# One decoder step on one core: two w_in chunks on tokens without their norm, pre-added squares, and 28 convolution taps placed in the inversion

## The reference, cut to what matters

```python
def rms_norm(x, g):
    xf = x.astype(jnp.float32)
    y = xf * lax.rsqrt(jnp.mean(xf * xf, axis=-1, keepdims=True) + NORM_EPS)
    return (y * g.astype(jnp.float32)).astype(x.dtype)

def conv_group(p, buf, dw_w, dw_b, ln_g, ln_b):
    u = p[..., :CONV_WIDTH] * jax.nn.sigmoid(p[..., CONV_WIDTH:])
    ext = jnp.concatenate([buf.astype(u.dtype), u], axis=1)
    c = lax.conv_general_dilated(ext, dw_w[:, None, :], ...) + dw_b
    ...

def layer(x, mk, mv, prev, s0, buf, lw):
    h = rms_norm(x, lw['g_mix'])
    p = h @ lw['w_in']
    rw, new_prev, new_s = rwkv7_group(p[..., :RW_PROJ], prev, s0, ...)
    cv, new_buf = conv_group(p[..., RW_PROJ:], buf, ...)
    x = x + jnp.concatenate([rw, cv], axis=-1) @ lw['w_out']
    x = x + cross_attn(rms_norm(x, lw['g_xattn']), mk, mv, lw['w_q'], lw['w_o'])
    x = x + moe(rms_norm(x, lw['g_moe']), ...)
    return x, new_prev, new_s, new_buf
```

## Time and profile before

| what | us |
|---|---|
| median of 3 runs | 1334.15 |
| lowest and highest | 1333.44 and 1334.32 |
| the profiled execution | 1333.15 |
| its span, first to last instruction | 1331.4 |
| PE busy / DVE busy / ACT busy | 1276.5 / 405.4 / 190.4 |

### The profile page before, as it was taken

One profiled execution on the slowest core, in us unless ns is written; L12 is line 12 of the kernel. 1 busy time (PEld: TensorE's weight loads), 2 busy tenths in 40 slices (PEclk: granted clock), 3 DMA queues, 4 the chain that ended last, 5 costly groups with the idle time before them and its releaser, 6 DMA issues.

```text
span 1331.4 us, 18885 instructions
## 1 busy us (share of the span) xinstructions
PE 1276.5 (96%) x8184; PEld 635.4 (48%) x8184; DVE 405.4 (30%) x820; ACT 190.4 (14%) x351; POOL 16.1 (1%) x39
## 2 busy tenths in 40 slices
PE   7999999999999999999999999999999999999995
PEld 5777865677784434434344333433333343443332
DVE  3998624532122121221312213112121311212122
ACT  3015222321221000100001000010100000010002
POOL 0002000000000000000000000000000000000000
PEclk9999999999999999999999999999999999999998
DMA  7335131285997999999999999999999999999995
GB/s 251 135 112 133 54 129 64 100 350 198 415 367 313 429 414 427 428 428 427 429 429 427 428 429 428 429 428 428 430 428 429 428 428 429 429 428 428 428 426 206
DMA packets 40280, 464.25 MB, mean 349 GB/s; under 512 B 8528, under 2 KB 10128, under 8 KB 12064
## 3 DMA queue, kind: packets, MB, share of 16 engines
q1 hardware_dynamic: 39392, 459.53, 83.2%
q0 software_dynamic: 832, 3.90, 0.9%
HBM read 458.34 MB, written 5.07 MB: 348 GB/s over the span
## 4 chain that ended last, share of the span: by engine, by line
PE 64%; DMA 26%; DVE 7%; ACT 1%; issue 0%; SPq 0%; DVEq 0%
PE ps L1109 32%; PE ps L567 20%; DMA arena<-in_w_gate 13%; DMA ring<-in_w_gate 10%; PE ps L1177 4%; DVE arena L1499 4%; DMA ring<-in_w_down 2%; PE ps L1133 2%; PE ps L1120 2%; DVE ring L1496 1%; PE ps L1126 1%; PE ps L1211 1%; PE ps L1167 1%; DVE arena L1496 1%; PE ps L1138 1%; DVE ring L1499 1%
## 5 line engine op out<-in xcount | busy, mean ns | idle before, releaser
L1109 PE MATMUL ps<-ring,xT 128*64 128x512 f32 x1536 | 342.7, 596 | 8.3 <-DMA ring<-in_w_up 5.5
L567 PE MATMUL ps<-arena,ring 128*128 128x288 f32 (+2 forms) x1152 | 231.4, 371 | 0.0
L1109 PEld LDWEIGHTS ps<-ring,xT 128*64 128x64 f32 x1536 | 105.9, 137 | 235.1 <-issue 208.4
L567 PEld LDWEIGHTS ps<-arena,ring 128*128 128x128 f32 (+1 forms) x1152 | 179.4, 176 | 45.8 <-issue 4.5
L1109 PE MATMUL ps<-ring,arena 128*64 128x512 f32 x768 | 171.7, 596 | 10.0 <-DMA ring<-in_w_down 10.0
L1253 ACT ACTIVATE arena<-ps 128x512 f32<-128x512 f32 (+5 forms) x136 | 76.3, 569 | 599.3 <-PE ps L1126 330.8
L1109 PE MATMUL ps<-arena,xT 128*64 128x512 f32 x512 | 115.5, 595 | 3.1 <-DMA arena<-in_w_gate 3.1
L1109 PEld LDWEIGHTS ps<-ring,arena 128*64 128x64 f32 x768 | 53.2, 137 | 111.2 <-issue 97.4
L1921 DVE TENSOR_SCALAR xT<-ps 128x512 f32<-128x512 f32 x32 | 22.1, 692 | 185.3 <-PE ps L1109 185.3
L1109 PEld LDWEIGHTS ps<-arena,xT 128*64 128x64 f32 x512 | 35.6, 137 | 74.3 <-issue 66.8
L1876 DVE TENSOR_TENSOR xT<-ps,vec 128x1024 f32<-128x1024 f32 x15 | 18.4, 1225 | 171.6 <-PE ps L1138 171.6
(11 more groups left out here) (218 smaller groups left out, 791.9 us busy)
## 6 DMA issues: line engine op xcount, KB each, us to landing
ring<-in_w_up SPq DMA_DIRECT2D x64, 2048.0 KB, 31.9
ring<-in_w_down SPq DMA_DIRECT2D x47, 2048.0 KB, 31.5
ring<-in_w_gate SPq DMA_DIRECT2D x32, 2048.0 KB, 34.2
arena<-in_w_gate SPq DMA_DIRECT2D x32, 2048.0 KB, 34.3
arena<-in_w_down SPq DMA_DIRECT2D x16, 2048.0 KB, 34.8
ring<-in_w_in SPq DMA_DIRECT2D x4, 2048.0 KB, 12.1
ring<-in_cache_k SPq DMA_DIRECT2D x4, 2048.0 KB, 17.8
ring<-in_cache_v SPq DMA_DIRECT2D x4, 2048.0 KB, 8.7
```

The costliest lines, as they stand in the source:

```text
L567: return nc.tensor.matmul(out, lhsT, rhs, start=start, stop=stop)
L1109: last = nc.tensor.matmul(out[AT[h ^ swap], :], lhs(k), part(weights(i), 0, 4, D)[:, k % 4, h * 512:(h + 1) * 512], start=(fresh and k == ...
```

## The change

- `W_IN_ORDER` begins 14, 15, 18, 19 in place of 14, 18, 15, 19.
- PE starts with twelve products of ones by ones, 128x128, into a bank that nobody reads.
- The first two chunks (14 and 15) are multiplied on `xg`, and `unit(1)` multiplies its gate by the norm's factor as `unit(0)` does.
- DVE adds the squares of the eight slices down to two (`x_sum`, three additions of 128x576), and `squares(1)` is two products in place of eight. It stands after the second product of chunk 15 (`between`). For the memory tokens two additions (128x1024, 128x512) bring eight slices down to two, and `squares(2)` is two products and stands after the third chunk in place of after the first.
- SP loads the weights of the first and second chunk as transfers of their own: chunk 14 goes ahead of the second half of the tokens, then chunk 15, then the other two.
- Taps 17 to 30 of channel blocks 2 and 3 leave their place before `shift(0, 4)` and go into the inversion, after levels 0 to 3: 8, 8, 6 and 6 instructions (`LATE_TAPS`).
- The rest renumbers semaphores. ACT's square for the key norm waits for the 100 convolution steps that then come before it.

The core of the diff:

```diff
+LATE_TAPS = (17, 21, 25, 28, 31)
-W_IN_ORDER = (14, 18, 15, 19, ...)
+W_IN_ORDER = (14, 15, 18, 19, ...)
...
+            for _ in range(12):
+                mm(ps[:, 5, 0:P], ones, ones)
+
-            def squares(n, src, w, bank):
-                pe.wait_ge(S["sq_done"], n)
+            def squares(n, need, src, w, bank):
+                pe.wait_ge(*need)
                 take(bank)
-                for k in range(KT):
+                for k in range(2):
...
-            squares(1, mix, TOK, 6)
...
+                linear("w_in", n, hT, TOK, range(8), "p_ps", 4 * n, p_reader, 4 if n < 5 else 2, steps=("h_done", KT + 2), raw=None if n else xg,
+                       between=lambda: squares(1, (S["h_done"], KT + 1), x_sum, TOK, 6),
+                       after=lambda m: squares(2, (S["mem_h"], 1), mem_sq, MEM, 7) if m == 2 else None)
...
             dve.wait_ge(S["x_in"], 16)
-            dve.wait_ge(S["x_in2"], 32)
-            for k in range(KT):
+            dve.wait_ge(S["piece2"], 16)
+            for k in range(4):
                 tell("h_done", v.tensor_scalar(xg[:, k, :], xT[:, k, 0:TOK], V("g_mix", k), None, MUL), False)
+            dve.wait_ge(S["sq_done"], 1)
+            tell("dve_c", tt(x_sum, mix[:, 0:2, :], mix[:, 2:4, :], ADD), False)
+            dve.wait_ge(S["x_in2"], 16)
+            for k in range(4, KT):
+                tell("h_done", v.tensor_scalar(xg[:, k, :], xT[:, k, 0:TOK], V("g_mix", k), None, MUL), False)
+            dve.wait_ge(S["sq_done"], 2)
+            link(tt(mix[:, 4:6, :], mix[:, 4:6, :], mix[:, 6:8, :], ADD))
+            tell("h_done", tt(x_sum, x_sum, mix[:, 4:6, :], ADD), False)
...
+            dve.wait_ge(S["sq_done"], 3)
+            link(tt(mem_sq[:, 0:4, :], mem_sq[:, 0:4, :], mem_sq[:, 4:8, :], ADD))
+            tell("mem_h", tt(mem_sq[:, 0:2, :], mem_sq[:, 0:2, :], mem_sq[:, 2:4, :], ADD), False)
...
-                if j == 0:
-                    link(tt(tmp2[:, 0, 0:TOK], tmp2[:, 0, 0:TOK], rs[:, :], MUL))
+                if j < 2:
+                    link(tt(tmp2[:, j, 0:TOK], tmp2[:, j, 0:TOK], rs[:, :], MUL))
...
-            conv((2, 3), 0, 17)
+            conv((2, 3), 0, LATE_TAPS[0])
...
-            conv((2, 3), 17, TAPS)
...
                 if 2 <= l + 2 < len(LEVELS):
                     mask_level(l + 2)
+                if l + 1 < len(LATE_TAPS):
+                    conv((2, 3), LATE_TAPS[l], LATE_TAPS[l + 1])
```

More of the change, by code:

```diff
@@ L208, in build @@
         rs_mem = arena[:, 16536:16792]
+        mem_sq = part(arena, 4352, KT, MEM)
+        x_sum = part(arena, 18104, 2, TOK)
         taps_of = [part(arena, at, NB, NT, TAPS) for at in (15544, 16824)]
@@ L567, in mm, with linear @@
                 return nc.tensor.matmul(out, lhsT, rhs, start=start, stop=stop)
-            def linear(name, n, src, width, banks, done, first, reader, tiles=4, steps=None, after=None, raw=None, ready=None):
+            def linear(name, n, src, width, banks, done, first, reader, tiles=4, steps=None, after=None, raw=None, ready=None, between=None):
                 i, f = front_fill(name, n)
                 for m in range(tiles):
-                    if m == 0 and raw is not None:
-                        pe.wait_ge(S["piece0"], 16)
-                    elif m == 0 or m == 1 and raw is not None:
+                    raws = 2 if raw is not None else 0
+                    if m < raws:
+                        pe.wait_ge(S[("piece0", "piece1")[m]], 16)
+                    elif m == raws:
                         pe.wait_ge(slot_in[i], 16 * (f + 1))
@@ L584, in linear @@
                             w = part(ring, i * SLOT, KT, 128 * tiles)[:, k, m * P:(m + 1) * P]
-                        if steps and n == 0 and (m == 0 or m == 1 and raw is not None):
-                            pe.wait_ge(S[steps[0]], steps[1] + m * KT + k)
+                        if m == 0 and raws:
+                            pe.wait_ge(S["h_done"], 1 + k)
+                        if steps and n == 0 and m == raws:
+                            pe.wait_ge(S[steps[0]], steps[1] + k)
                         if ready and first + m == 0 and k in ready:
                             pe.wait_ge(*ready[k])
-                        x = raw if m == 0 and raw is not None else src
+                        x = raw if m < raws else src
                         last = mm(ps[:, b, 0:width], w, x[:, k, 0:width], k == 0, k == KT - 1)
+                        if between and first + m == 1 and k == 1:
+                            between()
                     last.then_inc(S[done], 1)
@@ L596, in _ @@
             pe.wait_ge(S["pool_i"], 1)
-            def squares(n, src, w, bank):
-                pe.wait_ge(S["sq_done"], n)
+            for _ in range(12):
+                mm(ps[:, 5, 0:P], ones, ones)
+            def squares(n, need, src, w, bank):
+                pe.wait_ge(*need)
                 take(bank)
-                for k in range(KT):
-                    last = mm(ps[:, bank, 0:w], ones, src[:, k, :], k == 0, k == KT - 1)
+                for k in range(2):
+                    last = mm(ps[:, bank, 0:w], ones, src[:, k, :], k == 0, k == 1)
                 last.then_inc(S["sum_ps"], 1)
                 readers[bank] = [("root", n)]
-            squares(1, mix, TOK, 6)
             def p_reader(i):
@@ L883, in group_square @@
             def group_square(late):
-                pe.wait_ge(S["sq_done"], 6 if late else 5)
+                pe.wait_ge(S["sq_done"], 7 if late else 6)
                 group_sums(1, late, tsq, 7 if late else 4)
@@ L985, in _ @@
             for n in range(2):
-                linear("w_q", n, hT, TOK, range(8), "q_ps", 4 * n, lambda m: ("q_out", m + 1), steps=("h_done", 2 * KT + 1),
+                linear("w_q", n, hT, TOK, range(8), "q_ps", 4 * n, lambda m: ("q_out", m + 1), steps=("h_done", 2 * KT + 2),
                        after=lambda m: None if m else x_squares())
@@ L1104, in multiply @@
                     if pieces and 4 <= k < 7:
-                        pe.wait_ge(S[f"piece{k - 4}"], r * 16 + (32 if k == 4 else 16))
+                        pe.wait_ge(S[f"piece{k - 4}"], r * 16 + 32)
                     elif k == 0 or k == 4 or pieces and k == 7:
@@ L1257, in _ @@
             act.wait_ge(S["x_in"], 16)
-            a.activation(mix[:, 0:4, :], xT[:, 0:4, 0:TOK], ACT.Square)
-            act.wait_ge(S["x_in2"], 32)
+            tell("sq_done", a.activation(mix[:, 0:4, :], xT[:, 0:4, 0:TOK], ACT.Square), False)
+            act.wait_ge(S["x_in2"], 16)
             tell("sq_done", a.activation(mix[:, 4:, :], xT[:, 4:, 0:TOK], ACT.Square), False)
@@ L1269, in _ @@
             act.wait_ge(S["mem_in"], 16)
-            tell("sq_done", a.activation(part(arena, 4352, KT, MEM), memT, ACT.Square), False)
+            tell("sq_done", a.activation(mem_sq, memT, ACT.Square), False)
             inv_root((S["sum_ps"], 2), rs_mem, ps[:, 7, 0:MEM], 1.0 / D, 0)
@@ L1554, in conv @@
                         tell("conv", last, False)
[L1555 removed]
+                        taps_made[0] += 1
+                        taps_done[c] = taps_made[0]
             def conv_sample(c):
```

28 lines of the change are left out of this document (14 added, 14 removed).

## The result

| | median us | runs | ratio to before, 95% interval |
|---|---|---|---|
| before | 1333.80 | 1333.38 to 1334.32, 4 runs | |
| after | 1353.12 | 1352.58 to 1354.15, 4 runs | 1.0147 [1.0131, 1.0163] |

What follows compares the result with a forecast made beforehand. Full DMA weight stream bounds the end, so only its start, set by PE's and DVE's front, can move: 1333.15 - 8.6 = 1324.5, plus 1.0 for the median, 1325.5 us; range 1324 to 1327.5, with rivals 1323 to 1330 (0.85).

Steps and rivals of the forecast that it cites:

- From that release on, nothing but bytes counts: After PE's first slot release at 406.62 us, the expert weight stream alone sets the time; only its start can move.
- the sum's 1333.15 - 8.6: Whole kernel: profiled execution's time less the earlier lora products' gain, 1324.5 us; median forecast 1325.5.
- my slower rival: PE's new pauses at the start lose the clock; with any other delay, ending above 1334, chance 0.08.
- Early products and the clock: Kernel start: 24 rows of products of ones take 5.3 us and raise the clock, so chunk 14 runs at full pace.
- Rival 1: Start: products of ones don't raise the clock, or late; squares end 2.6 us later, gain 6.0, 1328.1; chance 0.11.
- Rival 4: Start: PE's pauses near 6.4, 8.4, 15.3 and 19.3 us lose the clock; with other delays above 1334, chance 0.08.
- Transfers: First loads: piece 14 at 6.4, second token half at 7.96, piece 15 at 9.3; additional transfer priced at nothing, at most 0.5.
- Start: PE's first chunks: squares end 12.35, norm 14.85, wait 1.2, 19 chunks from 21.4; lora products at 95.2, 8.6 us earlier.
- DVE in time: Up to `prep`: with 28 taps moved, DVE keeps up; `shift(0, 4)` waits until about 80.2; the 0.92 us wait stays.
- both bounds: Up to `prep`: PE's chunks with the small chain behind, and DVE's convolution, almost coincide; unmoved taps would limit the gain to 5.8.
- Taps in the inversion: Tap blocks of 3.2 and 2.4 us fit DVE's idle time, leaving 1.6 to 2.7; priced at nothing, 11.2 if uncovered.
- From `prep` to the release: Stretch before the first slot release: moves along with the earlier front, putting the first release near 398.

Runs made afterwards that it cites:

- before_pad6: The kernel before with six tiny memsets at the start of VectorE's program and nothing of the change: 1362.39 us, ratio 1.0214.
- before_pad7: The kernel before with seven tiny memsets at the start of VectorE's program and nothing of the change: 1334.50 us, ratio 1.0003.
- no_ones: after_pad1 without the 12 products of ones ahead of the first chunk: 1329.55 us.
- after_pad1: The changed kernel with one more tiny memset (128x1, private tile) at the start of VectorE's program: 1328.21 us, ratio 0.9952.
- runs 5 and 6: 5: the kernel before with only the 28 taps spread over the inversion, 1333.64 us; 6: after_pad1 with the 28 taps in their old place, 1328.77 us.
- after_pad1b: Repeat of after_pad1, the changed kernel with one more tiny memset, on another occasion beside other kernels: 1326.16 us.

## Why the prediction was wrong, point by point

- **The end.** "From that release on, nothing but bytes counts" is the step that failed, and with it the sum's 1333.15 - 8.6, which leaves what lies behind the last result as it was. It holds up to the last result (918.9 us after the release in after, 918.6 before). Behind it VectorE's skipped loop costs 27.2 us more, for fetches of code: its head lies across the border of two blocks. I took "what lies around" the work as fixed and moved it along, and counted added instructions by their own duration only. None of the rivals has it; my slower rival named another mechanism.
- **Early products and the clock.** The forecast has chunk 14 at full pace from its first product, since PE has by then worked some 5 us; that is my estimate from the one profile of before, whose squares run at half pace for 4.9 us. Right in after (24 rows in 4.51 us, forecast 5.3; the rows of chunk 14 are 0.24 us apart) and in four of the five other profiles with early products. But the 5 us are one reading of a moment that moves: the record of the clock begins 2.8 to 6.1 us after PE's first product (before_pad6, before_pad7), and the same 24 rows take 4.35 to 5.42 us. Rival 1's price, 2.6, is of the right size: 2.5 in no_ones. In after_pad1 `prep` is 1.95 later than in after, but 0.85 of that is the later piece. Rival 4, the clock lost in pauses, shows in that profile alone, and costs 1.4 and 1.6 us there.
- **Transfers.** First piece in use at 6.37 (forecast 6.4), second token half at 8.47 (7.96): half a us late. In all seven profiles with the new queue it is late, in use at 8.15 to 9.04, so the price of nothing for the additional transfer, or the pace of bytes that I took, is too low by 0.2 to 1.1 us. No run takes that transfer away, so how much of this is its doing stays open. The piece's landing moves from profile to profile, 6.2 to 7.6, which I hadn't allowed for.
- **Start.** The product behind the squares of tokens starts at 12.88 (forecast 12.35), norm at 15.37 (14.85), the wait ahead of the memory squares 0.78 (1.2), 19 chunks from 21.91 (21.4). The half us is the token half's, and the gain at the lora products is 8.06 in place of 8.6.
- **DVE in time.** Right: `shift(0, 4)` waits 5.56 us and starts at 80.88 (80.2); the 0.93 us wait for `prep` stays; runs 5 and 6 show both bounds at their prices, 0 and 5.7.
- **Taps in the inversion.** Right. DVE's timeline, which answers to the earlier trace rows (5.14 and 4.77 before):

```profile
157.48 1.47 DVE L1507 TENSOR_TENSOR ring<-ps,const 128x256 f32<-128x256 f32 x4 [1.97 <-PE ps L571]
...
160.00 3.25 DVE L1510 SCALAR_TENSOR_TENSOR arena<-arena,vec 128x256 f32<-128x256 f32 x8
164.85 1.47 DVE L1507 TENSOR_TENSOR ring<-ps,const 128x256 f32<-128x256 f32 x4 [1.61 <-PE ps L571]
...
172.23 1.47 DVE L1507 TENSOR_TENSOR ring<-ps,const 128x256 f32<-128x256 f32 x4 [2.40 <-PE ps L571]
```

  It is still idle 1.6 to 2.4 us ahead of these levels, as forecast (1.6 to 2.7), and 3.8 ahead of the last; the levels stay 7.38 us apart.
- **From `prep` to the release.** Forecast: moves along. In after 1.34 of the 8.06 are lost. The trace has the place:

```profile
131.95 2.25 PE L571 MATMUL ps<-arena,ring 64*64 64x128 f32 x32
...
133.68 1.22 DVE L1507 TENSOR_TENSOR ring<-ring,const 128x256 f32<-128x256 f32 x3 [2.93 <-PE ps L571]
134.90 1.15 PE L571 MATMUL ps<-const,ring 64*64 64x64 f32 x32 [0.70 <-ACT arena L1264]
```

  PE's product is 0.33 us longer than before (2.25 for 1.92), and then it waits. A packet on queue 8 at 132.10 took 1.77 us; that it is the cause isn't shown. after_pad1 has the same PE program and doesn't lose this (DVE's idle time there is 1.48), so it isn't a fixed price of the change. Whether a smaller one hides here is open: the stretch takes 272.4 to 274.4 us with the change and 272.6 to 273.5 without it.
- **Sum.** Without the split head the forecast holds in size: 1326.16 (0.9945 [0.9933, 0.9957]) and 1328.21 (0.9952 [0.9936, 0.9969]) against 1325.5 forecast, a gain of 7.4 and 6.0 against the medians of before on their chips (forecast 8.6). The first lies in the forecast's 1324 to 1327.5, the second in the wider 1323 to 1330. In the undisturbed profile of after_pad1b the span is 8.4 us under before's; but that execution is the fastest of its six, 1.4 us under their median.

## What to carry to other kernels

Count where code lies, not only what it does: adding a few instructions ahead of a loop that jumps over a long body can put its head across a fetch border, and each turn then costs some 9 us (here with a body of 278 instructions). Put one condition around such a loop, so that it is passed by one jump. When a profile's last stretch has no busy engine, look at the instruction packets and at the branch records before looking for a reason in the work; and when two bounds lie on top of each other, move both or neither.

## What the hardware showed that I had not expected

- VectorE's code comes in blocks of 128 instructions (packets of 8 KB; a tail with 6 and with 134 added instructions, none with 7, 70 and 110). Running across the border ahead of the first jump costs 0.46 us, VectorE's first jump over the body 3.1 to 4.6 us, and a split head some 2.3 + 3.7 + 3.4 us a turn. A split end cost nothing in the one profile that has it.
- A difference of one 0.06 us instruction moved the time by 25 us (1353.12 to 1328.21), by six 28 us (1334.18 to 1362.39).
- One program's profiles differ by 3.8 us of span (1326.7 and 1322.9), and three pieces make up the difference: 0.9 from the landing of one transfer, 1.4 and 1.6 from two falls of the granted clock (to 0.50, 3.41 us each). A part of this size can't be read from one profile.
